# A two-layer attention and expert kernel: gate products move into the attention stage, expert work is ordered tile by tile

## The reference

```python
def hybrid_layer(x, ...):
    (sb_q, ..., merge_g) = jnp.split(x @ w_in, split_points, axis=-1)   # 908 columns + 3 x 1024 gate columns
    o_sb, o_nsa, o_moba = three attention branches, 4 heads of 32 each
    g = jax.nn.sigmoid(merge_g).reshape(B, S, 3, D)
    mix = g[:, :, 0] * (o_sb @ w_br_sb) + g[:, :, 1] * (o_nsa @ w_br_nsa) + g[:, :, 2] * (o_moba @ w_br_moba)
    x = layer_norm(ALPHA * x + mix @ w_out, ln1_g, ln1_b)
    return layer_norm(ALPHA * x + peer_ffn(x, ...), ln2_g, ln2_b)

def peer_ffn(x, ...):    # per token: 4 heads x 8 = 32 experts of 16384, picked by two top-8 lists
    act = gelu(einsum('thkd,td->thk', u_tab[idx], xb))
    return einsum('thk,thkd->td', g * act, v_tab[idx])
```

## Time and profile before

| what | value |
|---|---|
| time, median of 3 runs | 3177.78 us (3175.78, 3177.78, 3189.7) |
| span of the profiled execution, first to last instruction | 3152.4 us |
| PE busy | 2495.9 us, 79% |
| DVE busy | 2024.9 us, 64% |
| POOL busy | 1266.6 us, 40% |
| ACT busy | 719.9 us, 23% |
| mean granted TensorE clock | 0.835 |
| moved by DMA | 701 MB, 222 GB/s |

### The profile page before, as it was taken

The page is one execution under the profiler, slowest core; times in us unless marked ns, Lnnn a source line. Parts: engine busy times, 40 slices in busy tenths (PEclk is TensorE's granted clock), DMA queues, the critical chain, the costliest instruction groups (busy, mean ns, idle before and its releaser), DMA issues.

```text
span 3152.4 us, 26183 instructions
## 1 busy us (share of the span) xinstructions
PE 2495.9 (79%) x8800; PEld 1224.7 (39%) x8800; DVE 2024.9 (64%) x4136; ACT 719.9 (23%) x1506; POOL 1266.6 (40%) x1028
## 2 busy tenths in 40 slices
PE   7889989878899998988789877988887888766000
PEld 4434434443333443453234333533332656544000
DVE  0221121547888666557878786568998767777888
ACT  2551001234444010134421101233444111000000
POOL 0000000114656442324675553126666533665575
PEclk9689999967879999995699988957888999878555
DMA  3001121436768674657789867447778867997697
GB/s 159 31 1 60 60 79 75 161 112 195 243 222 291 239 279 164 250 195 223 263 302 335 316 213 270 185 150 253 260 263 280 317 262 292 378 350 290 236 356 287
DMA packets 164581, 701.26 MB, mean 222 GB/s; under 512 B 18400, under 2 KB 18400, under 8 KB 156384
## 3 DMA queue, kind: packets, MB, share of 16 engines
q0 software_dynamic: 147456, 536.94, 49.1%
q1 hardware_dynamic: 14256, 152.28, 12.4%
q10 hardware_dynamic: 2736, 10.38, 0.8%
HBM read 691.13 MB, written 8.39 MB: 222 GB/s over the span
## 4 chain that ended last, share of the span: by engine, by line
PE 53%; DVE 19%; DMA 10%; POOL 8%; issue 7%; ACT 2%; DVEq 0%; ACTq 0%; PEldq 0%; SPq 0%
PE ps L504 13%; POOL rows L463 8%; PE ps L518 7%; PE ps L539 7%; PE ps L666 6%; PE ps L587 5%; DVE y L1057 5%; DVE rows L1043 4%; DMA rows<-in_table_v,idx 3%; DMA rows<-in_table_u,idx 3%; PE ps L700 2%; PE ps L725 2%; PE ps L743 2%; PE ps L599 2%; PE ps L506 2%
## 5 line engine op out<-in xcount | busy, mean ns | idle before, releaser
L463 POOL DMA_INDIRECT rows<-in_table_u,idx x512 | 629.2, 1229 | 1321.6 <-DVE idx L1150 702.8
L463 POOL DMA_INDIRECT rows<-in_table_v,idx x512 | 637.1, 1244 | 549.5 <-DVE y L1057 411.4
L504 PE MATMUL ps<-xT,wring 128*128 128x512 f32 (+1 forms) x1920 | 704.2, 522 | 59.7 <-DVE scratch L1193 22.7
L1057 DVE SCALAR_TENSOR_TENSOR y<-rows,wts,y 128x1024 f32<-128x1024 f32 x512 | 656.7, 1283 | 91.4 <-DMA rows<-in_table_v,idx 53.9
L1043 DVE CUSTOM_DVE_ANT_0 rows<-rows,x 128x1024 f32<-128x1024 f32 x512 | 614.8, 1222 | 68.2 <-DMA rows<-in_table_u,idx 65.0
L504 PEld LDWEIGHTS ps<-xT,wring 128*128 128x128 f32 x1920 | 376.4, 198 | 372.4 <-issue 295.7
L666 PE MATMUL ps<-KA,QA 33*128 33x512 f32 (+7 forms) x576 | 311.0, 672 | 63.4 <-DVE negm L1293 33.2
L518 PE MATMUL ps<-wring,scratch 128*128 128x512 f32 x512 | 234.3, 621 | 72.9 <-DVE scratch L1193 43.5
L539 PE MATMUL ps<-xT,wring 128*128 128x512 f32 (+1 forms) x640 | 230.7, 523 | 7.7 <-ACT xT L828 3.8
L1189 DVE SCALAR_TENSOR_TENSOR scratch<-scratch,ps 128x512 f32<-128x512 f32 (+1 forms) x120 | 69.3, 577 | 257.4 <-ACT scratch L820 257.3
L700 PE MATMUL ps<-QA,KA 64*128 64x512 f32 x408 | 205.5, 781 | 9.6 <-ACT scratch L943 9.6
(11 more groups left out here) (168 smaller groups left out, 2296.4 us busy)
## 6 DMA issues: line engine op xcount, KB each, us to landing
wring<-in_merge SPq DMA_DIRECT2D x30, 2304.0 KB, 10.5
wring<-in_w_out_h SPq DMA_DIRECT2D x10, 2048.0 KB, 10.2
wring<-in_w_query SPq DMA_DIRECT2D x10, 2048.0 KB, 11.8
x_row<-in_x SPq DMA_DIRECT2D x16, 512.0 KB, 8.3
wring<-in_attn_a SPq DMA_DIRECT2D x4, 2048.0 KB, 8.7
rows<-in_table_u,idx POOLq DMA_INDIRECT x512, 5.8
rows<-in_table_v,idx POOLq DMA_INDIRECT x512, 6.2
x_row<-x_mid SPq DMA_DIRECT2D x16, 512.0 KB, 9.1
```

Of the source, the lines that this page charges most:

```text
L463: pool.indirect_dma_start(rows[:, n % GATHER_SLOTS, :], None, tab_u if first_half else tab_v, bass.IndirectOffsetOnAxis(ap=idx[:, GT * (g ...
L504: pe.matmul(bank(k % 4)[:, 0:W], wg[:, c, P * c4:P * (c4 + 1)], xT[:, c, toks], start=(c == 0), stop=(c == KC - 1))
L1057: v.scalar_tensor_tensor(out=y[:, :], in0=row, scalar=wts[:, t, e:e + 1], in1=y[:, :], op0=ALU.mult, op1=ALU.add).then_inc(row_used, 1)
```

## The change

It does these things.

1. **Gate products in the attention stage.** The list `STEPS` gets 96 steps `gate` (24 gate products of 8 matmuls, each in four pieces of two), placed evenly over the five phases. All write PSUM bank 6; ACT copies each finished one raw into the new tile `G` in SBUF. The merge stage now has 24 branch products alone; ACT takes tanh of `G` in place. The gates of the last group are computed once, 512 tokens wide, for both halves.
2. To free bank 6, the stick-breaking scores rotate over two banks in place of three, so `stick` of block m+2 now waits for ACT's exponential of block m.
3. **Ring.** `wring` stays a ring of two, of 1 MB items (256 columns). `w_out` comes in four quarters: the first two are used for all tiles, then each tile gets its last two; PE waits for both of these before the first tile is finished. To make room, `x_row`, `ln1_gb`, `ck_sh` and `cv_sh` lie inside `scratch`, so rows for the residual and the norm's factors are loaded after attention; 64 rows of the compression inputs are kept in `KA` between groups.
4. **Expert sum in place.** `y` is gone: with weights divided by ALPHA, the sum is added into `x1`. L1040 and the wait for the store of the tile before go; now DVE writes a tile's `x1` in the first norm only after the store of the tile four before.
5. **Experts tile by tile**: u0, u1, v0, u2, v1, u3, v2, v3. The second half of a norm (and of the gelu) comes three steps into the next block.
6. `shares` is replaced by `expert_shares`, which walks all stages with planned PE and DVE costs and places a step where it fits, or where it is due before the first norm. Steps in each stage, before and after:

| stage | g1 before | g1 after | g2 before | g2 after | g3 before | g3 after |
|---|---|---|---|---|---|---|
| projection | 4 | 32 | 6 | 32 | 5 | 32 |
| attention | 154 | 200 | 104 | 147 | 190 | 200 |
| merge (first half) | 63 | 0 | 93 | 0 | 39 | 0 |
| first norm (first half) | 9 | 24 | 22 | 77 | 6 | 18 |
| query (first half) | 26 | 0 | 31 | 0 | 16 | 6 |
| second half: merge, norm, query | | | | | 82, 12, 34 | 0, 18, 19 |
| left for the end | | | | | 128 | 219 |

The diff, cut to its core:

```diff
-ITEM = 9 * 512
+ITEM = KC * 256
+RING = 2
+GATES = 24
+GATE_PARTS = 4
+def gate_steps(phase):
+    lo, hi = GATES * phase // (GT + 1), GATES * (phase + 1) // (GT + 1)
+    return [("gate", k, part, 1.72) for k in range(lo, hi) for part in range(GATE_PARTS)]
 def merged_steps(half):
-        streams = []
+        streams = [(gate_steps(phase), 1.0)]
...
+def expert_blocks(sec):
+    _, t0, nt = SECTIONS[sec]
+    out = [("u", t0)]
+    for t in range(t0 + 1, t0 + nt):
+        out += [("u", t), ("v", t - 1)]
+    return out + [("v", t0 + nt - 1)]
...
+        if kind == "ln1":
+            T = tiles_before(s) + n
+            if T >= GT:
+                nxt = max(nxt, due[T - GT])
+        while nxt < ready and max(busy, started) + EXPERT_US <= now + EXPERT_AHEAD:
+            busy = max(busy, started) + EXPERT_US
+            nxt += 1
...
+EXPERT_US, EXPERT_AHEAD = 1.45, 3.0
...
 # PE, attention
+                    if kind == "gate":
+                        k = GATES * g + t
+                        if a == 0:
+                            if t % 2 == 0:
+                                wg = slot(head_item(g, 4 + t // 2)).rearrange("p (c n) -> p c n", c=KC)
+                            if t >= 1:
+                                pe.wait_ge(gate_copied, k)
+                        for c in range(KC * a // GATE_PARTS, KC * (a + 1) // GATE_PARTS):
+                            mm = pe.matmul(bank(6), wg[:, c, P * (t % 2):P * (t % 2 + 1)], xT[:, c, :],
...
-                        if M >= 3:
-                            pe.wait_ge(sb_w, M - 2)
+                        if M >= 2:
+                            pe.wait_ge(sb_w, M - 1)
 # PE, out
+                for q in range(2):
+                    slot(tail_item(sec, 2 + q))
+                    for tt in range(nt):
+                        mm = out_columns(q, tt)
+                    mm.then_inc(out_half, 1)
+                    pe.wait_ge(out_half, 2 * sec + q + 1)
                     pe.nop().then_inc(item_used, 1)
+                for q in (2, 3):
+                    slot(tail_item(sec, 2 + q))
+                for tt in range(nt):
+                    out_columns(2, tt)
+                    out_columns(3, tt).then_inc(out_done, 1)
 # ACT, merge
-                    act.wait_ge(merge_done, k + 1)
-                    nc.scalar.activation(gate_buf[k % 4][:, 0:nt * P], bank(k % 4)[:, 0:nt * P], ACT.Tanh, scale=0.5)\
+                    raw = G[:, k6 % 3, k6 // 3, P * t0:P * (t0 + nt)]
+                    nc.scalar.activation(raw, raw, ACT.Tanh, scale=0.5).then_inc(gate_sig, 1)
 # DVE, v step
+                    y = x1[:, t, :]
+                    v.scalar_tensor_tensor(out=y, in0=row, scalar=wts[:, t, e:e + 1], in1=y,
+                                           op0=ALU.mult, op1=ALU.add).then_inc(row_used, 1)
 # DVE, first norm
+                    if T >= GT:
+                        dve.wait_ge(y_stored[T % GT], 16 * (T // GT))
+                    dve.wait_ge(out_done, T + 1)
```

More of the change, by code:

```diff
@@ new lines, in points @@
+def points():
+    out = []
+    for g in range(NG):
+        out += [("proj", g, n) for n in range(6)]
+        out += [("step", g, n) for n in range(len(STEPS[g % 2]))]
+        for sec, (sg, t0, nt) in enumerate(SECTIONS):
+            if sg == g:
+                out += [("merge", sec, k) for k in range(24)]
+                out += [("ln1", sec, t) for t in range(nt)]
+                out += [("query", sec, j) for j in range(8)]
+                out += [("route", sec, t) for t in range(nt)]
+    return out
@@ L865, in _ @@
                 g0 = GW * half
+                if half == 1:
+                    act.wait_ge(kept, g // 2 + 1)
+                    for r in range(NH):
+                        dst = slice(HD * r, HD * (r + 1))
+                        nc.scalar.copy(ck_sh[dst, 0:GW - r], c_kept[0:HD, r:])
+                        nc.scalar.copy(cv_sh[dst, 0:GW - r], c_kept[HD:2 * HD, r:])
                 for j in range(6):
@@ L954, in _ @@
                         b = lbuf[M % 2]
[L955 removed]
+                        after(nc.scalar.activation(b, bank(4 + M % 2), ACT.Abs))
                         after(nc.scalar.activation(b, b, ACT.Exp, scale=-1.0))
@@ L1321, in _ @@
                         section(sec)
-            expert_gates(len(SECTIONS) - 1)
-            expert_steps(len(SECTIONS) - 1, range(steps_of(len(SECTIONS) - 1)))
+            for at in SHARES["rest"]:
+                expert_step(*EXPERT_STEPS[at])
 def kernel(**inputs):
```

501 lines of the change are left out of this document (261 added, 240 removed).

## The result

The changed kernel takes 3220.39 us (median of 4 runs, 3210.07 to 3222.83), the kernel before 3181.37 us beside it (4 runs, 3175.78 to 3189.7): a ratio of 1.011, interval 1.0072 to 1.0148. It is slower by 1.1%. The forecast was 3090, range 3015 to 3180: wrong in sign and outside the range. A second set on another chip, against the kernel before on that chip, gave 1.0142 (1.0096 to 1.0188).

What follows compares the result with a forecast made beforehand. PE was taken as the limit in attention, DVE close behind in groups 1 and 3. Attention and merge -27 -63 -82 -32, norms +18 +100 +14, end -16: -88 from 3152.4, 3064; plus 25.4, 3090 us, range 3015 to 3180.

Steps and rivals of the forecast that it cites:

- Attention: Four attention stages with gate pieces: 290, 460, 300 and 460 us, in all 1510, against 1380 at full PE clock.
- 32 for the weights: Start of each attention stage: PE waits for the first gate weights, 8 us each, 8 x 4 in all.
- Rival C: Attention stages: the clock does not rise, mean 0.87, 156 us more than 1510, so 3246 us; chance 0.12.
- rival B: Attention of groups 1 and 3: DVE sets the pace, about 3140 us, 3186 at worst; chance 0.20.
- Rival A: Attention: PE and DVE fill better, 60 us of loss in place of 130, about 3020 us; chance 0.20.
- Merge stages: Merge of each group: DVE is the limit, 32 us full and 22 half-width, bounds 27 and 42.
- The rule of the Trainium skill: Merge: PE waiting between short bursts starts slow; each full merge up to 42 us, three of them 30 more.
- First norms: Out to query: group 0 stays at 76 us, group 1 +18, group 2 +100, section 3 +14.
- The end: After section 3's routing: 137 us, then 219 steps with norms and gelus in 329; 471 taken, -16.
- Rival D: End of the kernel: steps are only moved, 126 us longer there, nothing gained, 3170 us; chance 0.06.
- The 25.4 us outside the span: Whole kernel: median of the runs lies 25.4 us above the span, added to 3064 to give 3090.
- The slower side: Whole kernel: outcome slower than before, above 3194 us; chance 0.13.

Runs made afterwards that it cites:

- The two dense runs: Planned cost of an expert step 1.25 us in place of 1.45, with at most 31 or 16 projection steps, against the changed kernel: 3210.84 and 3202.78 us.

## Why the prediction was wrong

**The projection (77 us of the 157).** The step that failed is the one not taken: the table of the change says that 32 steps stand in each projection in place of 4 to 6, and the sum has no term for it. I costed that at nothing, without naming what hides them. Two things cost: ACT's queue, in which a gelu that waits for DVE stands ahead of copies that PE waits for (20 to 23 us at L677), and the gathers' traffic, beside which what PE needs next comes late. They overlap: with the first cured 6 to 10 us a projection come back, 26 in the three, and with the second cured on top of it another 12 and 17 in groups 2 and 3. That the traffic itself costs the time, and not what DVE's earlier steps change with it, is argued from that run and not separated. I had asked of added waits what is queued behind them, but only of the one that the change names.

**Attention.** Right in its mechanism and nearly in its sum: 305, 452, 314 and 454 us, together 1525, against 1510 with 32 for the weights, which fell into the projection's stretch, so 1478. The mis-sized term is the gate product's price: busy time by clock is 291, 424, 291 and 422, together 1428 us, not 1380, since a product in four pieces costs some 7.5 us and not 6.95. The loss over that ideal was 97 us, where I had 98 without the weights. So 47 us of the 157 lie here, 22 of them in group 0 and 21 in group 2. Rival C (the clock stays low) is refuted by 0.97 to 0.99; rival B's figure of DVE is right (369 us busy in group 1, forecast 370), but at 82% of the stage it didn't yet set the pace. The two dense runs show that it does 35 us later. Rival A's 60 us of loss were not reached.

**Merge stages.** 29, 29, 29 and 19 us against 32, 32, 32 and 22: DVE is their limit, as forecast. The rule of the Trainium skill that the prediction names ("TensorE: Matmul & The Clock Gate", section "HAM oscillation — how this bites in real kernels"), by which a PE that waits between short bursts drops to the slow clock, was applied to stages that have no long wait. The granted clock there was 0.99, 1.00, 0.92 and 0.97, but PE's waits for DVE between the products were 0.4 us at most in all four (group 2, the one with 0.92, has besides a wait of 4.0 us for ACT), so these rows don't speak for or against the rule. The half merge of section 4, costed at 22 us like that of section 3, holds a long wait, and took 33:

```profile
PE ps L567 <- DVE G L1301: 14.8, 1, 14.8
2715.00:2748.00 33.00, 15.26 (x49) 10.18 (x48) 31.19 (x122) 8.02 (x26) 5.90 (x6) 0.73 0.55 184
```

By windows of 3 us the granted clock is 0.50 (1.2 GHz) in the last 9 us of this wait, still 0.50 in the first 5 us after it with PE busy, and 1.00 again from 2739 on. That agrees with the rule.

**First norms.** Group 2's out to query was forecast at 188 and took 193: the working held, and with it the largest loss that I had seen coming. Group 0 was put at "76 as before" and took 75. That the timeline before has 67 from the first out product is only a shift: there PE waited 8.7 us for `w_out` ahead of that product, now it waits 6.4 us for it among them.

**The end.** 219 steps in 335 us, forecast 329, at a DMA share of 0.93. Ahead of them, section 4's own part was too short in my sum: PE's waits from 2700 on are

```profile
PE ps L581 <- DMA wring<-in_w_out_h: 10.7, 1, 10.7
PE ps L614 <- DMA wring<-in_w_query: 8.9, 2, 8.4
```

of which the second was not counted. From the end of section 3's routing (2731) to the end of section 4's (2886) it took 155 us where the sum has 137. Rival D's direction (the steps at the end are not paid for by the shorter stretch) is thus half right: +4 and not -16.

**The 25.4 us outside the span.** The sum adds them to get from span to median. The timed executions show 1.8 to 3.0; the rest was the distance of that one execution from the median. With 1.8 the same sum gives 3066.

**The slower side.** I gave it 0.13, nearly all of it to the clock. Half of the miss came from a place that no rival named, so that no weighing of the rivals could have put it right.

## What to carry to other kernels

A planner that fills a stage with background work must be costed on every engine that takes part: here ACT's and the DMA engines' share of a step, not DVE's alone. Where a block of steps ends inside a stage, look at what its last instruction, which waits, stands ahead of in each queue. And background work that fits one stage by its engine's slack should be set stage by stage: the same higher density gained 46 us in the norm of group 2 for 13 in its attention, and cost 43 and 45 us in the attention of groups 1 and 3.

## What was not expected of the hardware

- With the DMA engines' share at 0.96, small products of PE came with gaps of 1.0 to 1.15 us without a releaser; with a share of 0.59 in the same stretch there were none, and the first gate weights were waited for 10.4 and 7.9 us in place of 12.3 and 22.2. In one of the stages with full gathers there were no gaps either.
- PE's clock in attention depends on the piece size both ways: 0.95 with pieces of four matmuls, 0.98 with two, 0.94 with one (group 1, one trace each).
- Between chips the kernel before differed by 1% (3159 to 3192 us), as much as the effect of the change, and one kernel's ratio to it by 0.5%; only kernels on one chip could be set against one another.
